# Rebuilding the convolution stage of a two-block transformer kernel: float32 input weights, taps in PSUM, modulation by quarters

## The reference

```
mod = silu(c) @ mod_w + mod_b            # D x 6D weights, one row of input
sh1, sc1, g1, sh2, sc2, g2 = split(mod, 6)
h = rms_norm(x) * (1 + sc1) + sh1
u = h @ w_in + b_in                      # D x 2D
a, gt = split(u, 2);  u = a * sigmoid(gt)
u = causal depthwise conv(u, 31 taps) + dw_b
u = silu(layer_norm(u))
x = x + (1 + g1) * (u @ w_out + b_out)   # D x D
```

## Time and profile before

| | |
|---|---|
| median of 3 runs | 2885.38 us (2885.27 to 2885.8) |
| profiled execution, first to last instruction | 2885.3 us |
| busy PE, DVE, ACT, POOL | 2545.5, 1905.7, 1188.8, 834.8 us |
| granted PE clock, mean | 0.952 |
| loaded | 644.70 MB, mean 223 GB/s |

### The profile page before, as it was taken

The page is one execution under the profiler, slowest core; times in us unless marked ns, Lnnn a source line. Parts: engine busy times, 40 slices in busy tenths (PEclk is TensorE's granted clock), DMA queues, the critical chain, the costliest instruction groups (busy, mean ns, idle before and its releaser), DMA issues. The chain is left out here.

```text
span 2885.3 us, 30137 instructions
## 1 busy us (share of the span) xinstructions
PE 2545.5 (88%) x11100; PEld 2072.3 (72%) x11100; DVE 1905.7 (66%) x1958; ACT 1188.8 (41%) x1526; POOL 834.8 (29%) x335
## 2 busy tenths in 40 slices
PE   1675667487999999999988999998989999999998
PEld 1554555365888888888866878876768888888886
DVE  6769899887777677776756323259457755555545
ACT  2343333343534434444444445443444433443443
POOL 4665665376222222222222333443410000000000
PEclk9888888688999999999989999999989999999999
DMA  8774544376888888888874455678658866666664
GB/s 322 257 247 152 162 155 158 102 238 227 276 283 310 295 300 305 294 300 292 295 187 137 133 168 149 193 259 301 212 177 281 284 199 193 187 190 192 191 192 139
DMA packets 307393, 644.70 MB, mean 223 GB/s; under 512 B 30000, under 2 KB 63440, under 8 KB 306224
## 3 DMA queue, kind: packets, MB, share of 16 engines
q1 hardware_dynamic: 305984, 642.09, 68.2%
q0 software_dynamic: 448, 0.43, 0.1%
q10 hardware_dynamic: 816, 0.26, 0.0%
HBM read 640.60 MB, written 2.10 MB: 223 GB/s over the span
## 5 line engine op out<-in xcount | busy, mean ns | idle before, releaser
L85 ACT ACTIVATE whi<-stage 128x1024 fp32r<-128x1024 f32 x816 | 863.0, 1059 | 1242.2 <-PE bank L85 927.6
L85 DVE TENSOR_TENSOR wlo<-stage,whi 128x1024 fp32r<-128x1024 f32 x556 | 693.1, 1247 | 696.3 <-ACT whi L85 677.3
L85 POOL TENSOR_TENSOR wlo<-stage,whi 128x1024 fp32r<-128x1024 f32 x260 | 697.8, 2690 | 1136.1 <-ACT whi L85 1052.4
L85 PE MATMUL bank<-whi,hhi 128*128 128x512 f32 x2272 | 927.2, 408 | 78.6 <-POOL wlo L85 35.1
L85 PE MATMUL bank<-wlo,hhi 128*128 128x512 f32 x2272 | 901.4, 397 | 0.0
L85 PE MATMUL bank<-whi,hlo 128*128 128x512 f32 x2272 | 901.3, 397 | 0.0
L85 PEld LDWEIGHTS bank<-whi,hhi 128*128 128x128 f32 x2272 | 437.7, 193 | 191.0 <-issue 37.9
L85 PEld LDWEIGHTS bank<-whi,hlo 128*128 128x128 f32 x2272 | 436.5, 192 | 95.1
L85 PEld LDWEIGHTS bank<-wlo,hhi 128*128 128x128 f32 x2272 | 438.0, 193 | 91.9 <-issue 3.4
L85 PE MATMUL bank<-whi,ulo 128*128 128x512 f32 x992 | 390.1, 393 | 0.0
L85 PE MATMUL bank<-whi,uhi 128*128 128x512 f32 x992 | 389.6, 393 | 0.0
(11 more groups left out here) (106 smaller groups left out, 1156.0 us busy)
## 6 DMA issues: line engine op xcount, KB each, us to landing
stage<-in_mlp_w SPq DMA_DIRECT2D x256, 512.0 KB, 5.4
stage<-in_mod_w SPq DMA_DIRECT2D x192, 512.0 KB, 5.2
stage<-in_w_ada SPq DMA_DIRECT2D x192, 512.0 KB, 5.1
stage<-in_w_in SPq DMA_DIRECT2D x136, 512.0 KB, 3.9
stage<-in_w_ffn_gate SPq DMA_DIRECT2D x88, 512.0 KB, 4.4
stage<-in_w_ffn_up SPq DMA_DIRECT2D x88, 512.0 KB, 4.4
stage<-in_w_ffn_down SPq DMA_DIRECT2D x88, 512.0 KB, 4.0
stage<-in_conv_w_in SPq DMA_DIRECT2D x128, 256.0 KB, 4.4
```

Source lines behind the costliest of these rows:

```text
L85: made = fn(*args, **kw)
```

## The change

- `conv_w_in` is no longer split. `consume` only notes where a tile landed (kind "n"), and `pe_tile` issues four float32 matmuls of 128x512 straight from the landing buffer, with float32 activations `hx`. The landing buffer is free when PE is done. There are twelve buffers (`NFIRST`) for this stage: `stage2` takes the place in which `whi` and `wlo` lie later.
- The quarters of x are scaled, transposed and copied to `hx` ahead of the modulation (`x_quarter`) and modulated in place (`modulate_quarter`).
- Modulation tiles come in pairs: a tile has 512 columns of the shift and the same 512 of the scale (`mod_pairs`), so that 16 tiles give a quarter of both. In memory a row of such a tile is two runs of 2 KB instead of one of 4 KB. Gates stay as they were (`gate_tiles`). The first quarter comes alone, each later one is mixed with six product tiles.
- The first 64 modulation tiles are all summed by DVE. The other 96 of block one that come in this stage are all `aside`: ACT and POOL alone. The ring `products_of` still has one buffer. 70 of them are mixed into the remaining 46 tiles of `conv_w_in`, 10 follow the third tile of `conv_w_out`, 16 are mixed into the rest.
- Taps: fourteen channel tiles on DVE, two (3 and 14) on PE. DVE sums in a PSUM bank, always in two chains in turn: two channel tiles, or one tile's taps 0 to 15 and 16 to 30. ACT copies the sums to CV. Up to nine steps of two taps are issued after each product tile.
- Value and gate stay in PSUM: `gated` lets ACT take the sigmoid, then one DVE instruction adds the bias and multiplies.
- The layer norm takes a provisional mean of 13 channel tiles, subtracts it and squares before the last three are ready, and corrects at the end.
- The residual parts of `conv_w_out` tiles (`wlo`) are all made by DVE; before, all by POOL. Modulation pairs are also used in the later stages.

```
@@ constants @@
-CONV_PE = (1, 0, 1, 0, 1, 0, 0, 1)
-SHARE = {7: (1, 3, 5, 7, 9, 11, 13), 8: (3, 8), 9: (3, 8)}
+NFIRST = 12
+N_MOD_IN = 70
+N_MOD_GAP = 10
-N_MOD_IN = 56
-N_MOD_GAP = 12
+TAPS_A_TILE = 9
+DVE_JOBS = ((0, 1), (2, 4), (5, 6), (7, 8), (9, 10), (11, 12), (13,), (15,))
+PE_JOBS = (3, 14)
+LN_LATE = (13, 14, 15)
@@ build_program: buffers @@
+        with nc.sbuf_tensor("stage2", [128, NFIRST - NSTAGE, 2, 512], F32) as stage2:
+            pass
+        with nc.sbuf_tensor("hx", [128, NKT, S], F32) as hx:
+            pass
@@ between_tiles @@
+            for _ in range(min(len(dve_taps), TAPS_A_TILE)):
+                dve_taps.popleft()()
+            if pe_taps:
+                pe_taps.popleft()()
@@ consume @@
+            if it["kind"] == "n":
+                it["c"]["done_tiles"][it["t"]] = (s, landed)
+                consumed[0] += 1
+                return
...
-                if m["shared"] and kt in SHARE.get(m["chunk"], (2, 6, 10, 14)):
-                    stage_free[s] = [mod_second(m, kt, w, c, landed)]
+                if m["aside"]:
+                    t = stage_free[s] = [mod_aside(m, kt, w, c, landed)]
@@ mod_aside (was mod_second) @@
+        def mod_aside(m, kt, w, c, landed):
...
             i, buf, free = products_of.take()
             t = A.put(nc.scalar.activation, buf, w, ACT.Copy, scale=c, after=[landed, m["cond"]] + free)
+            m["last"] = P.put(nc.gpsimd.tensor_tensor, m["buf"][1], m["buf"][1], buf, ALU.add,
+                              after=[t, m["last"]])
+            products_of.give(i, m["last"])
@@ x_quarter, modulate_quarter @@
+            scaled = scale_rows(q, first["rstd"])
+            for half in range(2):
+                b, bank, free = misc.take()
+                for k in range(2):
+                    for tok in range(2):
+                        kk = 2 * half + k
+                        t = T.put(nc.tensor.transpose, bank[:, k * 256 + tok * 128:k * 256 + tok * 128 + 128],
+                                  scaled[tok][1][:, kk * 128:(kk + 1) * 128], ident[:, :],
+                                  after=[scaled[tok][2], consts] + free)
+                kt = 4 * q + 2 * half
+                x_columns[kt] = A.put(nc.scalar.activation, hx[:, kt:kt + 2, :],
+                                      bank[:, :].rearrange("p (k n) -> p k n", k=2), ACT.Copy, after=[t])
+                misc.give(b, x_columns[kt])
+            cols = [mod_cols[(0, 0, q)], mod_cols[(0, 1, q)]]
+            for kt in range(4 * q, 4 * q + 4):
+                h, after = hx[:, kt, :], cols + [x_columns[kt - kt % 2]]
+                if kt % 2:
+                    t = A.put(nc.scalar.activation, h, h, ACT.Identity, scale=MC[:, 0, 0, kt:kt + 1],
+                              bias=MC[:, 0, 1, kt:kt + 1], after=after)
+                else:
+                    t = V.put(nc.vector.tensor_scalar, h, h, MC[:, 0, 0, kt:kt + 1], MC[:, 0, 1, kt:kt + 1],
+                              ALU.mult, ALU.add, after=after)
+                h_ready[kt] = [t]
@@ mod_pairs @@
+            w = a[("mod_w", "w_ada_2")[block]][0].rearrange("r (w n) -> r w n", w=6)
+            m = dict(block=block, norm=norm, q=q, pair=True, cond=(cond, cond2)[block], aside=aside, soon=soon)
+            if then is not None:
+                m["then"] = then
+            return [dict(kind="m", mod=m, t=t, src=w[128 * t:128 * (t + 1), 3 * norm:3 * norm + 2, 512 * q:512 * (q + 1)])
+                    for t in range(NKT)]
@@ pe_tile @@
+                if native:
+                    s, landed = c["done_tiles"][t]
+                    done[tok] = T.put(nc.tensor.matmul, pair[tok][:, :], hx[:, kt, tok * 128:(tok + 1) * 128],
+                                      slots[s][:, k, :], start=first, stop=last,
+                                      after=[landed] + c["ready"][kt] + (c["free"] if first else []),
+                                      signal=(k == 1 and (last_tile or tok == 1)))
+                    continue
@@ taps @@
+            chains = [(cts[0], 0, 16), (cts[0], 16, TAPS)] if len(cts) == 1 else [(ct, 0, TAPS) for ct in cts]
+            job = {}
+                for k, (ct, lo, hi_) in enumerate(chains):
+                    if lo + n < hi_:
+                        job["at"][k] = tap_dve(ct, lo + n, bank[:, k * S:(k + 1) * S], n == 0,
+                                               free if n == 0 else [job["at"][k]])
@@ order of the stream @@
-        seq += mod_tiles(0, 0, True) + mod_tiles(0, 2, True)
-        seq += mix(ci[0][0:4] + ci[1][0:4] + ci[2][0:4], mod_tiles(0, 1, True) + mod_tiles(0, 3, True))
+        early = [mod_pairs(0, 0, q, soon=True, then=lambda q=q: tasks.append(lambda: modulate_quarter(q)))
+                 for q in range(4)]
+        seq += early[0]
+        for q in range(3):
+            seq += mix([it for c in ci[0:3] for it in c[2 * q:2 * q + 2]], early[q + 1])
+        rest = ci[0][6:8] + ci[1][6:8] + ci[2][6:8]
+            mods += gate_tiles(0, 2, half, aside=True, then=lambda half=half: tasks.append(lambda: add_output_bias(half)))
+            mods += mod_pairs(0, 1, q, aside=True)
         seq += mix(rest, mods[:N_MOD_IN])
...
-                        residual_epilogue(q, 0, 2), pool=1)
-        seq += co[:2] + mods[N_MOD_IN:N_MOD_IN + N_MOD_GAP] + mix(co[2:], mods[N_MOD_IN + N_MOD_GAP:])
+                        residual_epilogue(q, 0, 2))
+        seq += co[:3] + mods[N_MOD_IN:N_MOD_IN + N_MOD_GAP] + mix(co[3:], mods[N_MOD_IN + N_MOD_GAP:])
@@ start, and between the two products @@
+        while consumed[0] < 14:
+            consume()
...
+        while len(pair_ready) < 2:
+            consume()
```

More of the change, by code:

```diff
@@ L404, in mod_end @@
                         b, bank, free = misc.take()
[L405 to L408, removed]
+                    t = T.put(nc.tensor.matmul, bank[:, :], ones[:, :], buf[:, (q % 2) * 512:(q % 2) * 512 + 512],
+                              start=True, stop=True, after=[made, consts] + free)
                     g = G[:, which // 3, q * 512:(q + 1) * 512]
@@ L413, in mod_end @@
             else:
[L414 to L431, removed]
@@ L432, in mod_end @@
-                mod_cols[(n, which % 3, 2 * half)] = mod_cols[(n, which % 3, 2 * half + 1)] = t2
-            misc.give(b, t2)
[L434 to L438, removed]
+                k, q = m["norm"], m["q"]
+                for j in range(8):
+                    t = T.put(nc.tensor.matmul, bank[:, j:j + 1], buf[:, j * 128:(j + 1) * 128], ones[:, 0:1],
+                              start=True, stop=True, after=[made, consts] + free)
@@ new lines, in dve_job, with pe_job, part @@
+            for n in range(0, steps):
+                dve_taps.append(lambda n=n: step(n))
+            dve_taps.append(end)
+        def pe_job(ct):
+            job = {}
+            def part(lo, hi_):
+                if lo == 0:
+                    job["bank"] = misc.take()
+                b, bank, free = job["bank"]
+                i, buf, free_t = tiles.take()
+                for j in range(lo, hi_):
+                    d = buf[:, 128 * (j - lo):128 * (j - lo + 1)]
+                    w = A.put(nc.scalar.activation, d, ident[:, :], ACT.Copy, scale=tap(ct, j),
+                              after=[consts] + [params[k] for k in tap_params] + free_t)
+                    t = T.put(nc.tensor.matmul, bank[:, 0:S], d, U[:, ct, j:j + S], start=(j == 0),
+                              stop=(j == TAPS - 1), after=[w, u_ready[ct]] + free)
+                tiles.give(i, t)
+                if hi_ == TAPS:
+                    conv_done[ct] = A.put(nc.scalar.activation, CV[:, ct, :], bank[:, 0:S], ACT.Identity,
+                                          bias=PA[:, 48 + ct:49 + ct], after=[t, params["A"]])
+                    misc.give(b, conv_done[ct])
+                    conv_finished(ct)
+            for lo in range(0, TAPS, 4):
+                pe_taps.append(lambda lo=lo: part(lo, min(lo + 4, TAPS)))
@@ L753, in start @@
+                        misc.give(two[1][0], r)
+                        misc.give(two[0][0], u_ready[ct])
+                        tiles.give(i, u_ready[ct])
+                        jobs_ready()
+                        for ct in (2 * p, 2 * p + 1):
+                            if ct in PE_JOBS:
+                                pe_job(ct)
+                    later(1, gated)
                 tasks.append(first)
             return start
-        def ln_sum(ct):
-            if ct == 0:
-                ln["mean"] = misc.take()
-            _, bank, free = ln["mean"]
-            ln["sum"] = T.put(nc.tensor.matmul, bank[:, 0:S], ones[:, :], CV[:, ct, :], start=(ct == 0),
-                              stop=(ct == NKT - 1), after=[conv_done[ct], consts] + free)
@@ L763, in build_program @@
-        s_ready = {}
-        def layer_norm():
-            A.put(nc.scalar.activation, ST[:, 61:62], eps, ACT.Sqrt, after=[consts])
-            b, bank, _ = ln["mean"]
-            im, mu, free = tiles.take()
```

(33 more changed lines are left out.)

420 lines of the change are left out of this document (230 added, 190 removed).

## The result

The changed kernel takes 2835.05 us (median of 4 runs, 2830.81 to 2835.51), the kernel before 2885.32 (4 runs): a ratio of 0.9828 (0.9814 to 0.9841), 50 us less. The prediction had the sign and its range holds the time, but it forecast 110 us less. The profiled execution is one of 2830.81 us with a span of 2829.0, so 4 us ahead of the median.

What follows compares the result with a forecast made beforehand. DVE was taken to set the pace up to the out product, then the ACT-POOL chain. Ends at 145, 423, 458 and 584 us, the last instead of 694.2, gave 2885.3 - 110 = 2775 us, range 2705 to 2845.

Steps and rivals of the forecast that it cites:

- Six such pairs cost 12 us: Input product: ACT waits some 4.5 us for each pair's last tap, POOL's add hides 2.4; six pairs cost 12 us.
- the 244 of the forecast: Input product after 145 us: 65 modulation tiles stepping at 3.76 us through ACT, the only product buffer and POOL, 244 us.
- moved ahead under the taps: Layer norm between the products: centring and squaring of 13 tiles is done under the taps, so 14 us stay of 25.6.
- The sign that the prediction named: Input product, 145 to 423 us: the forecast is wrong if POOL idles long between adds; the wait is then PE or DMA.
- Between the products: From input product to out product, 423 to 458 us: gating, last channel tile's taps, layer norm, two wlo; 35 us against 82.
- The out product: From 458 to 584 us: three tiles, ten modulation steps of 3.76 with PE idle about 30 us, then 29 tiles, 80 us.
- The early part: Start to 145 us: transfers and PE each reach about 135, 10 added for mutual waits; PE's first product tile at 57.
- rival 2: Whole kernel: delays add up, POOL slowed to its mean or taps at 0.73, MLP held by transfers; 2815 to 2860; chance 0.14.
- The time of 2799: Alternative total if PSUM taps are 65 ns dearer: a pair 4 us, six pairs 24 us in ACT's way; 2799.
- Rival 1: Input and out products: only the chain counts; bias, tap copies and the ten tiles lie in slack; about 2725; chance 0.17.
- Rival 3: Input product: PE stays at 1.2 GHz, a native tile takes 6.96 us, the stage ends at 585; 2937 us; chance 0.07.
- Rival 4: Early part and MLP: transfers of pairs slow them until the gain of 110 us is lost; no change; chance 0.04.

## Why the prediction was right in direction and wrong in size

**The step that failed** is "Six such pairs cost 12 us". The mechanism was seen, but the term was sized by a mean, with product tiles of equal spacing, which left ACT 4.5 us to wait per pair. In the trace the nine steps after a tile are issued together, so ACT reaches the copy after four or five products of 3.67 us, while DVE needs 25 us; in the case shown it waits 11.46. The whole stretch, from the first add at 160.46 to the 63rd at 468.49, taken apart:

- 62 steps of 3.66 are 226.9 us, with 10.7 ahead of the first (149.80 to 160.46) and 1.5 behind the last 239: the 244 of the forecast less 5.
- Output bias in POOL: twice 7.6 (the first from 250.56 to 258.15). As ACT writes its next product meanwhile, each makes a step only 6.25 longer, together 12.5 where 22 were put.
- The rest, 308.0 - 226.9 - 12.5 = 68.6, is POOL standing longer than its usual 1.32 us. Five pair copies: gaps of 12.69, 10.81, 3.09, 11.14 and 7.13, together 38 over the usual. Three other places, where ACT waited for PE (a chunk's sums, their transposes, the taps that PE makes): 13.85, 2.76 and 4.75, 17 over; in the first of them the copy of the first pair would have kept ACT just as long, as its last tap ended only then. The last three centring steps, where ACT waits for DVE before it squares: 12. Only the 12 us for taps had been planned.

One stop of each of the last two kinds, in the timeline of POOL:

```profile
195.32 2.34 POOL L80 TENSOR_TENSOR R<-R 128x1024 f32<-128x1024 f32 x1 [13.85 <-ACT R L80]
...
457.24 2.34 POOL L80 TENSOR_TENSOR R<-R 128x1024 f32<-128x1024 f32 x1 [8.39 <-ACT R L80]
```

So +57 - 5 - 10 = +42. The taps' part is shown: moving the copies off ACT gave 38 us. The other two are read from the trace and were not tried apart. Centring had been put at nothing, "moved ahead under the taps"; it is under DVE's taps, but it too stands in ACT's queue, ahead of products. The sign that the prediction named came: POOL idles long between adds. But the wait behind it was for the most part ACT's queue, and not PE or DMA as it said there.

**Between the products** 9 us too little. The gating began 3.8 us after the last input matmul, at 473.77, and the taps at 474.69, sooner than the 7 us put. But two more products and two whi stood in ACT's queue, and DVE's taps stopped from 478.0 to 483.5 for two wlo and a centring step. They were over at 494.4, and the 19 diagonals of the last PE job were then still to be built and multiplied; its result was copied at 504.34. I had DVE's job as the last, so these 10 us were not in the sum. The layer norm behind it took 9.3 us instead of 14. Read from the timeline, not tried.

**The out product** came out at 130 for 126, with its hole: ten adds in steps of 3.66 from 517.76 to 550.78, the fourth whi on ACT at 550.61.

**Right to within a few per cent:** the price of a native matmul (20 of them, two rows each, in 17.33 us, 0.87), the step of the chain (3.66 for 3.76), taps 0.40 apart that don't stretch, and the MLP, where runs of 2 KB cost nothing: what follows the out product took 2185 us, 2191 before. The early part was right in sum though PE began 7 us earlier than forecast.

```profile
254.66 17.33 PE L80 MATMUL bank<-stage,hx 128*128 128x512 f32 x40
```

That the range holds the time is luck in part: it reached that far for the sake of rival 2, whose mechanism did not come.

The Trainium skill's page "VectorE: DVE Perf Modes" (the TRN2 errata) would, by the estimate from its figures, have made a tap in PSUM 65 ns dearer. The trace does not agree: 60 taps in PSUM took 23.59 us, 0.39 each, and 16 in SBUF before 0.40 each, and single taps have medians of 481 and 472 ns; the measurement decides. The time of 2799 that I worked out by it was nearer to the result, for another reason.

The Trainium skill's page "SBUF — State Buffer", in the section "Who interferes with whom", says that a DVE instruction with two inputs in SBUF contends with a GpSimd instruction that reads SBUF, and that one with at most one, outside the 2-port modes, does not. The runs agree: beside POOL's adds a tap took a mean of 767 ns with the running sum in SBUF, 480 with it in PSUM.

**The rivals.** Rival 1 (the chain alone counts, 2725) is refuted: the waits in ACT's queue were not hidden in slack, and with the tap copies taken out of it, still with one buffer, the time is 2797. Rival 2 (delays add up, 2815 to 2860) has the measured time, but not its mechanism: in the input product POOL's adds stayed at 2.35 us and taps at 480 ns, while the delays were waits in ACT's queue. Rival 3: in the windows the granted clock was 0.86 from 150 to 300 us and 0.83 from 300 to 400, not near 0.5. One of rows 1 does not fit a clock that PE's activity lifts: from 25 to 50 us it was 1.00 with PE busy 5.5 of 25 us. Rival 4: nothing was lost in the MLP.

## What to carry to other kernels

When an engine is a link in a chain, price each other instruction in its in-order queue by when its input is done and when it is reached, not by a mean rate over the stage: here the copies, one per pair, cost three times their forecast (38 us for 12). Moving such waits to the engine that makes their input (the copy behind the last tap, on DVE) freed the chain here. A handoff through one buffer makes the two engines' times add up (3.66 us a tile); a second buffer brought it near POOL's add alone (2.5 us). The buffer was worth 46 us by itself and 52 with the queue wait removed as well.

## What the runs showed of the hardware

- A scalar_tensor_tensor of 128x256 that reads its running sum from PSUM beside a busy POOL never rose above 484 ns among those of 140 to 480 us. With the sum in SBUF the median was 472 and the mean 767: at least half were not stretched, and the longest was held to 2589 ns, about one add of POOL.
- The contention went both ways and unevenly: in that SBUF run most adds near 230 us kept 2.36 us while taps were stretched, but one add, otherwise 2.35 us long, was held to 11.54.
- 64 more float32 matmuls (56 us of PE) in a stage in which PE waited cost 9 us.
